# One 2048-wide model block pair on one core: job scores ahead of weight subtractions, mixed heads split one by one, 20 products moved, last gated down-projection joined

## The chip, the cores and the metric

One NeuronCore of a Trainium2 chip (trn2) runs the whole program. The metric is the device time of one execution in microseconds (us), lower is better.

## What is computed

The reference is two transformer blocks in float32 on 256 tokens of width 2048, one after the other.

```python
def reference(...):
    x = first_block(x, p, ...)
    return second_block(x, c_2, ...)

# first_block: three mixers side by side, then a gated feed-forward, then a gated projection of p
proj = rmsnorm(h) @ w_in                      # 2048 -> 4 hgrn heads, 6 fox heads, 6 moba heads of 128
h = h + concatenate([hgrn, fox, moba]) @ w_out
h = h + (gelu(conv(c @ w_gate)) * (c @ w_up)) @ w_down        # 5632 wide
h = h + sigmoid(e @ w_ple_gate) * (p @ w_ple_proj)
# second_block: modulated by silu(c) @ w_mod (12288 columns), 16 window heads of 64, 8 latent heads of 128
proj = (rmsnorm_2(x) * (1 + sc1) + sh1) @ w_in
x = x + g1 * (concatenate([swa, mla]) @ w_out)
x = x + g2 * (relu(h @ w_ff1) ** 2) @ w_ff2                   # 8192 wide
return rmsnorm_2(x)
```

## The kernel before, in words

**Split products.** Everything is feature-major: a block is 128 features by 256 tokens. Each weight is read once from HBM in units of 128 x 2048 float32 (1 MB), 384 of them, each of two halves of eight 128 x 128 tiles. ScalarE (ACT) rounds a half to fp32r (`rnd`, line 863, tile `wh`), VectorE (DVE) subtracts to get the low part (`sub`, line 1363, tile `wl`), both LOOK = 3 halves ahead of TensorE (PE) with four slots (HS = 4). Activations are split in the same way into a high and a low part (`his`, `hi_x` on ACT; `lo`, `lo_x` on DVE, lines 1493 and 1473). A tile costs PE two matmuls: high weights by the pair (512 columns, line 532) and low weights by the high part (256 columns, line 533), summed in a bank of 512 columns, of which DVE adds both halves to `x` (`add_blocks`, lines 1413 and 1415). The joined form (lines 525 to 527) makes three matmuls that sum in one half of the bank.

**The stages**, in order, with their units: A 16 (hgrn projections), B 19 (fox), C 18 (moba), out 8 and outb 8 (the two halves of `w_out`), ffn1 128 (gated feed-forward, a hardware loop of 48 halves four times in it), plep 2, down1 4 (the rest of `w_down`), pleg 16, in2 16, uq 3, ukv 2, out2 8 and out2b 8, ffn2 128.

**What runs between.** No scheduler is at work: each engine's queue is written out half by half, and semaphores join them. On DVE `half(before, after)` waits that PE has finished the half ahead, does `before` (taking the last block from PSUM), then `sub` for three halves on, then `after`. An attention job (one head) goes in steps, one step in a half, 48 steps in all: 9 in C for fox, 9 in out for moba, 19 in in2 and uq for the window heads (`swa`), 11 in out2 for the latent heads (`mla`). In a step (`job_step`) PE makes the scores of job j (line 589), the value product of j - 3 (line 598) and the transposes of j - 2 (line 607); DVE takes the scores and the maximum of j (lines 1550 to 1560) and scales the probabilities of j - 1 (lines 1567 and 1570); ACT copies out j - 3, copies the transposes of j - 2 and takes the exponential of j (line 995). All this is in `after` on DVE, behind `sub`.

**The mixed heads.** `w_out` reads `mix`, split into 16 pairs. Before `out`, ACT and DVE split the first eight at once; those eight pairs lie in `xs`, which C's products still read, so the split waits for the end of C. The last eight are split after the last job, between out and outb, and likewise in out2. The value blocks of moba are transposed by PE at the start of out, all three pairs (line 576).

**Products of the modulation.** `w_mod` is used by DVE alone: 192 products (`mods`, line 1431, 128 x 1024) of a 512 KB slice in one of two slots, each loaded by POOL's queue when the slot's last product is done.

## Time and profile before

| | |
|---|---|
| time, median of 3 runs | 2400.34 us (2397.83 to 2402.98) |
| the profiled execution | 2399.3 us, span 2397.6 us |
| granted TensorE clock, mean | 0.992 |
| PE busy | 2337.4 us (97%), 13766 matmuls |
| DVE busy | 1940.7 us (81%) |
| ACT busy | 1178.0 us (49%) |
| POOL busy | 109.0 us (5%) |
| read from HBM | 510.27 MB, 214 GB/s over the span |

The profile is of one execution. Busy times are unions of the instructions of an engine. The ends of matmuls are modelled, so the distance from one start to the next tells their pace. "Idle before" is put down to the engine that released the instruction last. Stages aren't marked in it; their places were found by counting the halves that PE finished.

### The profile page before, as it was taken

To read this page: it belongs to the slowest core of one execution; us is meant where nothing else is said; L and a number is where in the kernel's file an instruction comes from. 1 tells how busy PE (TensorE), PEld (TensorE's weight loads), DVE (VectorE), ACT (ScalarE), POOL (GpSimd) and SP (SyncE) were. 2 spreads that over 40 slices of the span, in tenths; PEclk is the share of its full clock that TensorE was granted. 3 is DMA by queue.
4 is the path that set the end of the run, shared out by engine and by line. 5 is a ranking of instruction groups with operands and counts; after the bars stand their busy time and mean duration, and the time that the engine had idled before them with its cause. 6 is when DMAs were issued, how large, how long until landed. Compare 5 with 4: busy or idle time off the path is not lost.

```text
span 2397.6 us, 38235 instructions
## 1 busy us (share of the span) xinstructions
PE 2337.4 (97%) x13766; PEld 2032.2 (85%) x13766; DVE 1940.7 (81%) x3144; ACT 1178.0 (49%) x1697; POOL 109.0 (5%) x208
## 2 busy tenths in 40 slices
PE   7999999999999999999999999999999999999997
PEld 6888787888888888888888897788988888888886
DVE  6987787889988889898989866778777777777777
ACT  5544444565545454454456666545644434434432
POOL 0000010001000000000000000000000000000000
PEclk9999999999999999999999999999999999999998
DMA  7456666458888878788775652436455545555552
GB/s 284 172 189 228 234 237 214 156 203 302 275 280 277 282 270 288 260 298 277 277 267 176 213 197 89 151 130 223 182 193 179 191 181 189 189 180 192 179 191 88
DMA packets 86244, 514.43 MB, mean 215 GB/s; under 512 B 9669, under 2 KB 10229, under 8 KB 36944
## 3 DMA queue, kind: packets, MB, share of 16 engines
q1 hardware_dynamic: 57312, 407.93, 47.6%
q0 software_dynamic: 28640, 104.24, 13.0%
q8 instruction: 95, 1.56, 0.3%
q14 instruction: 53, 0.43, 0.1%
q10 hardware_dynamic: 144, 0.26, 0.0%
HBM read 510.27 MB, written 2.13 MB: 214 GB/s over the span
## 4 chain that ended last, share of the span: by engine, by line
PE 89%; DVE 7%; ACT 2%; issue 2%; DMA 1%; SPq 0%; DVEq 0%; ACTq 0%; POOLq 0%
PE ps L532 46%; PE ps L533 23%; PE ps L530 4%; PE ps L525 2%; PE ps L526 2%; PE ps L527 2%; PE ps L529 2%; DVE wl L1363 2%; PE ps L589 2%; ACT wh L863 1%; PE ps L598 1%; DVE x L1415 1%; PE ps L617 1%; DVE modraw L1431 0%; PE ps L566 0%
## 5 line engine op out<-in xcount | busy, mean ns | idle before, releaser
L863 ACT ACTIVATE wh<-raw 128x1024 fp32r<-128x1024 f32 x768 | 810.7, 1057 | 728.9 <-PE ps L530 481.2
L1363 DVE TENSOR_TENSOR wl<-raw,wh 128x1024 fp32r<-128x1024 f32 x768 | 938.0, 1223 | 249.4 <-ACT wh L863 233.4
L532 PE MATMUL ps<-xs,wh 128*128 128x512 f32 x2907 | 1050.1, 402 | 19.7 <-DVE wl L1363 13.2
L533 PE MATMUL ps<-xs,wl 128*128 128x256 f32 x2907 | 817.9, 281 | 0.0
L532 PEld LDWEIGHTS ps<-xs,wh 128*128 128x128 f32 x2907 | 549.5, 189 | 150.2 <-DVE wl L1363 14.0
L533 PEld LDWEIGHTS ps<-xs,wl 128*128 128x128 f32 x2907 | 552.2, 190 | 10.2
L1431 DVE CUSTOM_DVE_ANT_0 modraw<-modraw,cb 128x1024 f32<-128x1024 f32 x192 | 233.2, 1218 | 4.4 <-DMA modraw<-in_wmod 4.4
L1415 DVE SCALAR_TENSOR_TENSOR x<-ps,mod,x 128x256 f32<-128x256 f32 x320 | 154.8, 484 | 88.4 <-PE ps L530 82.7
L532 PE MATMUL ps<-xc,wh 128*128 128x512 f32 x616 | 222.0, 399 | 0.0
L532 PE MATMUL ps<-hs,wh 128*128 128x512 f32 x608 | 218.8, 398 | 1.9 <-DVE x L1413 1.9
L533 PE MATMUL ps<-xc,wl 128*128 128x256 f32 x616 | 173.3, 281 | 0.0
L533 PE MATMUL ps<-hs,wl 128*128 128x256 f32 x608 | 170.6, 281 | 0.0
L532 PE MATMUL ps<-hs2a,wh 128*128 128x512 f32 x448 | 160.8, 398 | 1.6 <-DVE up L1388 0.8
L532 PE MATMUL ps<-hs2b,wh 128*128 128x512 f32 x448 | 161.0, 398 | 0.0
L525 PE MATMUL ps<-xd,wh 128*128 128x258 f32 x512 | 148.3, 290 | 3.9 <-DVE xd L1473 3.9
L526 PE MATMUL ps<-xd,wh 128*128 128x258 f32 x512 | 146.7, 287 | 0.0
L527 PE MATMUL ps<-xd,wl 128*128 128x258 f32 x512 | 145.2, 284 | 0.0
L470 POOL DMA_DIRECT2D modraw<-in_wmod x176 | 92.9, 528 | 1107.7 <-DVE modp L1431 616.2
L532 PEld LDWEIGHTS ps<-xc,wh 128*128 128x128 f32 x616 | 115.8, 188 | 28.5
L532 PEld LDWEIGHTS ps<-hs,wh 128*128 128x128 f32 x608 | 114.4, 188 | 26.3 <-issue 3.0
L533 PE MATMUL ps<-hs2a,wl 128*128 128x256 f32 x448 | 125.7, 281 | 0.0
L533 PE MATMUL ps<-hs2b,wl 128*128 128x256 f32 x448 | 125.7, 281 | 0.0
(286 smaller groups left out, 2983.0 us busy)
## 6 DMA issues: line engine op xcount, KB each, us to landing
raw<-in_w SPq DMA_DIRECT2D x383, 1024.0 KB, 5.0
modraw<-in_wmod POOLq DMA_DIRECT2D x192, 512.0 KB, 4.5
x<-in_x SPq DMA_DIRECT2D x4, 512.0 KB, 8.7
tbias<-rel_rows POOLq DMA_DIRECT2D x4, 512.0 KB, 6.0
out_dram<-mix SPq DMA_DIRECT2D x4, 512.0 KB, 2.6
raw<-in_w SPq DMA_DIRECT2D x2, 512.0 KB, 7.9
cb<-c_silu POOLq DMA_DIRECT2D x1, 1024.0 KB, 8.6
hmask<-in_hmask SPq DMA_DIRECT2D x1, 512.0 KB, 17.3
```

The costliest lines, as they stand in the source:

```text
L470: pool.dma_start(modraw[:, n:n + 1, :], a["wmod"][bass.ds(i * MOD_SLOTS + (MOD_SLOTS + n), 1), :, :] .rearrange("a p n -> p a n")).then_in ...
L525: nc.tensor.matmul(out[:, 0:N], hi[:, w], xh, start=s, stop=False)
L526: nc.tensor.matmul(out[:, 0:N], hi[:, w], xl, start=False, stop=False)
L527: m = nc.tensor.matmul(out[:, 0:N], lo[:, w], xh, start=False, stop=e)
L529: nc.tensor.matmul(out[:, 0:T], lo[:, w], xh, start=False, stop=False)
L530: m = nc.tensor.matmul(out[:, :], hi[:, w], pair, start=False, stop=True)
L532: nc.tensor.matmul(out[:, :], hi[:, w], pair, start=s, stop=e)
L533: m = nc.tensor.matmul(out[:, 0:T], lo[:, w], xh, start=False, stop=e, skip_group_check=e)
L863: nc.scalar.activation(wh[:, h % HS, :], raw[:, u % RAW, (h % 2) * 1024:(h % 2 + 1) * 1024], ACT.Copy).then_inc(s_round, 1)
L1363: nc.vector.tensor_tensor(wl[:, h % HS, :], raw[:, (h // 2) % RAW, (h % 2) * 1024:(h % 2 + 1) * 1024], wh[:, h % HS, :].bitcast(F32), ALU. ...
L1415: ins.append(nc.vector.scalar_tensor_tensor(x[:, k, :], b[:, q * T:(q + 1) * T], gate[:, k:k + 1], x[:, k, :], ALU.mult, ALU.add))
L1431: nc.vector.tensor_tensor_reduce(out=modraw[:, m % 2, :], in0=modraw[:, m % 2, :], in1=cb[:, (m % 2) * 1024:(m % 2 + 1) * 1024], scale=1.0 ...
```

## The change

DVE's `half` gets a third hook, `pre`, which runs ahead of `before` and of `sub`. All 48 job steps move there from `after`. The split of the mixed heads goes one by one: in C, two heads in each of four halves, into `xm`, a new place of 16 KB over the fox heads' projections; in out and out2 each head is split as its job ends, and the steps are packed into one half fewer. Moba's value transposes go to two halves of C and one of out.

Of the 192 products 20 leave C; each of the four loop turns in ffn1 takes 28 instead of 24, and 4 more are done in in2; the 8 of out2b go to out2. POOL's queue loads the first of the late ones ahead of its wait for the norm of in2. down1 is made with joined products, and DVE adds one 256-column half for a block instead of two.

```diff
-            def half(before=None, after=None):
+            def half(before=None, after=None, pre=None):
+                if pre:
+                    pre()
                 if before:
                     dve.wait_ge(s_used, c.val("h", c.n["h"]))
                     before()
                 sub(c.n["h"] + LOOK)
...
+            def add_joined(ks):
+                for k in ks:
+                    nc.vector.tensor_tensor(x[:, k, :], bank()[:, 0:T], x[:, k, :], ALU.add).then_inc(s_evac, 1)
+                dve.wait_ge(s_evac, c.n["b"])
...
+        xm = at("xm", [P, KB // 2, 2, T], 144, F32R)
-        XMIX = {"out": XPAIR, "out2": XPAIR[8:16] + XPAIR[0:8]}
+        XMIX = {"out": [xm[:, k, :, :] for k in range(KB // 2)] + XPAIR[8:16], "out2": XPAIR[8:16] + XPAIR[0:8]}
+        MOBA_V = {30: 0, 34: 1}
+        MIX_AT = 29
-        LATE_MODS = 14
+        LATE_MODS = 18
-        moba_steps = lambda i: share(C_H + JOB_LAG, i, MOBA_J, 2 * U_OUT)
+        moba_steps = lambda i: share(C_H + JOB_LAG, i, MOBA_J, 2 * U_OUT - 1)
+        out_taken = lambda steps, i: [j - JOB_LAG for j in steps(i) if j >= JOB_LAG]
...
-            fulls(U_C, keep(S1), lambda j: 1 + (j >= 3), fox)
+            fulls(U_C, keep(S1), lambda j: 1 <= j < 14, fox, jobs=fox_jobs)
...
+                if 0 < i - MIX_AT <= 4:
+                    for k in (2 * (i - MIX_AT) - 2, 2 * (i - MIX_AT) - 1):
+                        lo(XS["mix"] + k, XMIX["out"][k], mix[:, k, :])
...
-                unit("quad", hpairs(hs, CH_LAST), between=lambda q: early_sums(N_PLE, 2 * u + q, SUM_QUAD))
+                unit("quad", hpairs(hs, CH_LAST), between=lambda q: early_sums(N_PLE, 2 * u + q, SUM_QUAD), joined=True)
...
-                      nmod=1, m0=0)
-                downs(lambda: gate_in(CH - 1), lambda: conv(CH - 1), nmod=1, m0=CH)
-                units(CH, product, first=last_down(), h_lo_of=lambda j: h_lo(hs, j), nmod=1, m0=2 * CH)
+                      mod=lambda j: body_mods(1 + (j == 4)))
+                downs(lambda: gate_in(CH - 1), lambda: conv(CH - 1), mod=lambda j: body_mods(1 + (j == 4)))
+                units(CH, product, first=last_down(), h_lo_of=lambda j: h_lo(hs, j), mod=lambda j: body_mods(1 + (j in (1, 5))))
...
+                if 2 <= i < 10:
+                    mods(1)
...
+            def mla(i):
+                mods(i % 2)
+                for h in out_taken(mla_steps, i - 1):
+                    lo(XS["mix2"] + 8 + h, XMIX["out2"][8 + h], mix[:, 8 + h, :])
```

Three places in the queues, with line numbers of each kernel's own (1363 is 1390 in the change, 1550 is 1582, 1493 is 1525, 1396 is 1425). First DVE in late in2, from the weight subtraction ahead of the second reciprocal (of the latent norms) to the scores of a job; the number after `ps` is the bank of the scores, which alternates from job to job. Before:

```order
L1363 TENSOR_TENSOR wl_51<-raw_49,wh_50 128x1024
L1947 RECIPROCAL hvr_102<-hvr_102 128x256
L1493 TENSOR_TENSOR xs_56<-mix_57,xs_56 128x256
L1550 SCALAR_TENSOR_TENSOR prob_94<-ps5,tbias_54 128x128
L1550 SCALAR_TENSOR_TENSOR prob_94<-ps5,tbias_54 128x256
L1555 TENSOR_REDUCE small_77<-prob_94 128x1 x2
L1560 TENSOR_SCALAR small_77<-small_77,par_72 128x2
```

The same place in the change:

```order
L1390 TENSOR_TENSOR wl_51<-raw_49,wh_50 128x1024
L1999 RECIPROCAL hvr_103<-hvr_103 128x256
L1525 TENSOR_TENSOR xs_56<-mix_57,xs_56 128x256
L1582 SCALAR_TENSOR_TENSOR prob_95<-ps4,tbias_54 128x128
L1582 SCALAR_TENSOR_TENSOR prob_95<-ps4,tbias_54 128x256
L1587 TENSOR_REDUCE small_78<-prob_95 128x1 x2
L1592 TENSOR_SCALAR small_78<-small_78,par_73 128x2
```

The scores behind this subtraction were those of the same half (`ps5`) and are now those of the next (`ps4`): the job of the half has been done ahead of the subtraction.

Second DVE at the border of C and out, from the last of moba's head norms and products to the first adds of out. Before:

```order
L1431 ISA modraw_52,modp_75<-modraw_52,cb_53 128x1024
L1431 ISA modp_75 128x1
L1396 TENSOR_TENSOR tk_a_60<-ps0,tk_a_60 128x256
L1398 TENSOR_TENSOR sec_63<-tk_a_60,rstd_a_59 128x256
L1493 TENSOR_TENSOR xs_56<-mix_57,xs_56 128x256 x8
L1363 TENSOR_TENSOR wl_51<-raw_49,wh_50 128x1024
```

In the change:

```order
L1568 SCALAR_TENSOR_TENSOR sec_64<-sec_64,par_73,ps5 128x512
L1425 TENSOR_TENSOR tk_a_60<-ps0,tk_a_60 128x256
L1427 TENSOR_TENSOR sec_64<-tk_a_60,rstd_a_59 128x256
L1390 TENSOR_TENSOR wl_51<-raw_49,wh_50 128x1024
L1448 TENSOR_TENSOR x_55<-ps1,x_55 128x256 x2
```

The two products ahead of the last take of C and the eight splits behind it are gone from here.

Third DVE in down1, one half of it, from the adds to the sums of squares. Before:

```order
L1413 TENSOR_TENSOR x<-ps,x 128x256 x4
L1363 TENSOR_TENSOR wl<-raw,wh 128x1024
L1473 SCALAR_TENSOR_TENSOR xs<-x,par,xs 128x256 x2
L1502 TENSOR_TENSOR sq<-sq 128x512
L1506 TENSOR_TENSOR sqs<-sq 128x256
```

In the change:

```order
L1438 TENSOR_TENSOR x<-ps,x 128x256 x2
L1390 TENSOR_TENSOR wl<-raw,wh 128x1024
L1505 SCALAR_TENSOR_TENSOR xs<-x,par,xs 128x256 x2
L1534 TENSOR_TENSOR sq<-sq 128x512
L1538 TENSOR_TENSOR sqs<-sq 128x256
```

Two of the four adds of a half are gone.

## Rows read from the trace of the kernel before

**Rows 1.** The page: busy times, chain by engine, the products' group (busy us, mean ns, idle).

```profile
PE 2337.4 (97%) x13766; PEld 2032.2 (85%) x13766; DVE 1940.7 (81%) x3144; ACT 1178.0 (49%) x1697; POOL 109.0 (5%) x208
...
PE 89%; DVE 7%; ACT 2%; issue 2%; DMA 1%; SPq 0%; DVEq 0%; ACTq 0%; POOLq 0%
...
L1431 DVE CUSTOM_DVE_ANT_0 modraw<-modraw,cb 128x1024 f32<-128x1024 f32 x192 | 233.2, 1218 | 4.4 <-DMA modraw<-in_wmod 4.4
```

**Rows 2.** Windows: stretch, length, busy PE, PEld, DVE, ACT, POOL, PEclk, DMA share, GB/s.

```profile
780.00:840.00 60.00, 60.00 (x342) 52.15 (x341) 53.91 (x85) 24.28 (x27) 5.34 (x11) 1.00 0.80 278
1665.00:1725.00 60.00, 60.00 (x499) 59.89 (x499) 45.45 (x75) 41.79 (x70) 0.00 (x0) 1.00 0.52 194
398.40:405.20 6.80, 5.48 (x20) 4.72 (x20) 2.75 (x6) 2.43 (x4) 0.00 (x0) 0.50 0.73 243
1456.50:1459.90 3.40, 3.35 (x16) 3.35 (x17) 1.87 (x3) 2.36 (x6) 0.00 (x0) 0.50 0.01 2
1654.50:1661.30 6.80, 4.83 (x22) 4.83 (x23) 4.18 (x7) 5.79 (x7) 0.53 (x1) 0.50 0.27 84
```

**Rows 3.** Timeline of PE at the start of out: start, length in us.

```profile
397.38 1.09 PE L576 MATMUL ps<-ident,sec 128*128 128x128 f32 x8 [1.93 <-DVE sec L1398]
399.80 1.11 PE L576 MATMUL ps<-ident,sec 128*128 128x128 f32 x4 [1.32 <-ACT vt L975]
...
402.63 0.63 PE L532 MATMUL ps<-xs,wh 128*128 128x512 f32 x1
...
403.27 0.63 PE L532 MATMUL ps<-xs,wh 128*128 128x512 f32 x1
```

**Rows 4.** Waits of PE over the whole run: us in total, times, longest.

```profile
PE ps L532 <- DVE xs L1493: 2.9, 2, 1.5
```

**Rows 5.** Waits of PE, then of DVE, in 1440:1510 (late in2, uq).

```profile
PE ps L607 <- DVE prob L1570: 7.9, 6, 2.4
...
DVE wl L1363 <- ACT wh L863: 19.9, 13, 3.4
```

**Rows 6.** Timeline of DVE and PE around one of these waits.

```profile
1450.86 1.23 DVE L1363 TENSOR_TENSOR wl<-raw,wh 128x1024 fp32r<-128x1024 f32 x1 [1.50 <-ACT wh L863]
...
1454.12 0.61 DVE L1550 SCALAR_TENSOR_TENSOR prob<-ps,tbias 128x128 f32<-128x128 f32 x2
...
1456.55 0.90 PE L607 MATMUL ps<-ident,prob 128*128 128x128 f32 x3 [2.37 <-DVE prob L1570]
```

**Rows 7.** down1: waits of PE in 1243:1275; one group of DVE in 1243:1270.

```profile
PE ps L532 <- DVE x L1413: 1.9, 3, 1.4
PE ps L532 <- issue: 1.3, 1, 1.3
...
L1413 DVE TENSOR_TENSOR x<-ps,x 128x256 f32<-128x256 f32 x27 | 10.2, 417 | 0.2
```

**Rows 8.** Windows of DVE alone: busy, PEclk, DMA share, GB/s; out2b, out2, early in2.

```profile
1599.20:1646.90 47.70, 45.89 (x81) 1.00 0.61 210
1525.90:1599.20 73.30, 51.28 (x113) 1.00 0.38 130
...
1368.00:1394.00 26.00, 20.63 (x26) 1.00 0.89 317
```

**Rows 9.** Waits of PE in 1640:1665, the start of ffn2.

```profile
PE ps L525 <- DVE xd L1473: 3.9, 2, 2.5
```

**Rows 10.** Timeline of DVE and PE after a turn of the feed-forward loop.

```profile
737.30 0.42 DVE L1396 TENSOR_TENSOR tk<-ps,tk 128x256 f32<-128x256 f32 x1 [3.33 <-issue]
...
738.72 1.22 DVE L1363 TENSOR_TENSOR wl<-raw,wh 128x1024 fp32r<-128x1024 f32 x1
...
741.29 0.40 PE L532 MATMUL ps<-xc,wh 128*128 128x512 f32 x1
```

**Rows 11.** Timeline in out2: a weight subtraction, and the first matmul that reads it.

```profile
1562.74 1.23 DVE L1363 TENSOR_TENSOR wl<-raw,wh 128x1024 fp32r<-128x1024 f32 x1
...
1579.17 0.40 PE L532 MATMUL ps<-xs,wh 128*128 128x512 f32 x1
```

More of the change, by code:

```diff
@@ L672, in fox, with moba_v @@
                 head_norm(1, i - MOBA_N)
+                if i in MOBA_V:
+                    g = MOBA_V[i]
+                    pe.wait_ge(s_scl, SCALED["C"] + 2 * C_H + 2 * g + 2)
+                    if g == 0:
+                        pe.wait_ge(s_oe, J_MOBA)
+                    else:
+                        pe.wait_ge(s_hrms, 2)
+                    moba_v(g)
+            def moba_v(g):
+                for q in range(2):
+                    for t in range(2):
+                        m = nc.tensor.transpose(PS[7 - g % 2][:, (2 * t + q) * P:(2 * t + q + 1) * P],
+                                                sec[:, S1 + 2 * C_H + 2 * g + q, qt(t)], ident[:, :])
+                m.then_inc(s_vT, 1)
             for u in range(U_C):
@@ L1090, in fox @@
                 head_norm(1, S1, i - MOBA_N)
+                if i - 1 in MOBA_V:
+                    v_copy(3, MOBA_V[i - 1], 7 - MOBA_V[i - 1] % 2)
+                if 0 <= i - MIX_AT < 4:
+                    his("C", XMIX["out"][2 * (i - MIX_AT):], [mix[:, 2 * (i - MIX_AT) + k, :] for k in range(2)])
             for u in range(U_C):
@@ L1112, in eights @@
                 act.wait_ge(s_oe, jobs_done)
-                his(phase, XMIX[phase][8:], [mix[:, k, :] for k in range(8, KB)])
                 b = FIRST[phase][1] + KB
@@ L1303, in mla @@
                     job_step(J_MLA, mla_job, MLA_H, j)
-            eights("out2", None, J_END, mla, N_MLP2, "mlp2", "mix2", lambda: shift_hi(1, SH2))
+                for h in out_taken(mla_steps, i):
+                    act.wait_ge(s_oe, J_MLA + h + 1)
+                    his("out2", XMIX["out2"][8 + h:], [mix[:, 8 + h, :]])
+            eights("out2", J_END, mla, N_MLP2, "mlp2", "mix2", lambda: shift_hi(1, SH2))
             def ups2(buf, first=None):
@@ L1458, in eights @@
                         dve.wait_ge(s_oe, jobs_done)
-                    for k in range(8 if split else 8 * part, 8 * part + 8):
-                        lo(XS[name] + k, XMIX[phase][k], mix[:, k, :])
                     for i in range(2 * U_OUT):
                         half((lambda: add_blocks([i - 1], gate)) if i else None,
-                             after=lambda: (second(i) if part else between(i)))
+                             after=lambda: (second(i) if part else between(i)), pre=None if part else lambda: jobs(i))
                     tail(lambda: add_blocks([KB - 1], gate))
@@ L1967, in swa @@
                     job_step(J_SWA, swa_job, SWA_H, j)
-            fulls(U_IN2, lambda j: take_rstd("in2", j, rstd_b), lambda j: 1 <= j <= 4, swa, late=2)
+            fulls(U_IN2, lambda j: take_rstd("in2", j, rstd_b), between=swa, late=2, jobs=swa_jobs)
             def latent_take(n):
```

105 lines of the change are left out of this document (60 added, 45 removed).

## The prediction, written before the change was run

> **What bounds the kernel now.** I read the page first. TensorE (PE) is busy for 2337.4 of 2397.6 us, and 89% of the chain that ended last runs through it, so a microsecond counts only where PE stands still or runs slowly [rows 1]. Next came the windows. In the steady part of the gated feed-forward 342 matmuls, 171 pairs, fill 60 us: 0.351 us for a tile [rows 2]. That pace nothing in this change touches. What is left is the some 60 us in which PE has nothing to do, and the stretches at the lower clock. So I went through PE's waits in order of time and asked of each who releases it.
>
> Five places bear on the change. At the start of out PE stands 1.93 us, because its transposes need the last block of C, and 1.32 us more, because the third group needs a bank that ACT has to empty [rows 3]. Twice, at the middle of out and of out2, it waits for the split of mixed heads, 2.9 us together [rows 4]. In late in2 and in uq it waits six times for scaled probabilities, 7.9 us together, and there DVE itself stands 19.9 us waiting for ACT's rounding [rows 5]. In down1 it waits 1.9 us for adds, and 1.3 us for what the profile calls issue right behind them, where DVE makes its last adds too; I count both [rows 7]. At the start of ffn2 it waits 3.9 us for the low parts of the last two blocks [rows 9].
>
> **What the waits do to the clock.** The granted clock is 0.50, which is 1.2 GHz, in three stretches, 6.8, 3.4 and 6.8 us long, and each begins within or just behind one of these waits: 398.4 between the two at out, 1456.5 with the one of 2.37 us in late in2, 1654.5 with those of ffn2 [rows 2, 3, 6]. At that clock a pair takes 403.27 - 402.63 = 0.64 us, not 0.351 [rows 3], so 45% of PE's busy time there is lost: 0.45 x (5.48 + 3.35 + 4.83) = 2.5 + 1.5 + 2.2 = 6.2 us. I take it that the clock stays at 2.4 GHz once the wait ahead is gone. The Trainium skill, "TensorE: Matmul & The Clock Gate", in its terms, prices lower clock as the throttled time by one minus the ratio. By that the three stretches would be worth 8.5 us, 2.3 more than by the rows, where PE was partly idle.
>
> **The sum, part by part.**
>
> Start of out. The value transposes are spread, and the third group, which alone needs the last block, stands one half (2.8 us) after the end of C; DVE reaches that block at once, since the two products of 1.22 us ahead of it are gone [rows 1]. Both waits go, and the clock with them: 3.25 + 2.5 = 5.7 us. The work on PE is the same. In C ACT gets eight roundings more and DVE eight splits of some 0.42 us (what a 256-column operation takes in rows 10), in exchange for 20 products of 1.22 us: 24.4 us off DVE and 3.4 us onto it. Nothing there waits for longer.
>
> Mixed heads, the second eight. The last job ends in the half ahead of the border and its split is a matter of 0.4 us on each of two engines, with a half of PE's work over it: 2.9 us go. If the cover were gone, a head would cost PE 1 us.
>
> Late in2 and uq. Now DVE does the job of a half behind the subtraction, and the subtraction waits for a rounding that ACT can only do after the exponential of the job before. Rows 6 show it: the subtraction starts at 1450.86 after 1.50 us of idle time, behind it and a reciprocal the job's scores are taken at 1454.12, and PE gets its probabilities at 1456.55, 2.37 us late. With the job first this ring is cut: DVE waits for PE's scores alone, and the 19.9 us that it stood for ACT are spent behind the job. DVE's sum doesn't grow. But the two reciprocals of the latent norms and their followers still stand between two jobs, so I leave 2 us of the 7.9 standing (bounds: 0 and 4). Gain: 5.9 + 1.5 = 7.4 us.
>
> down1. DVE makes half the adds; 27 of them took 10.2 us, so some 5 us are taken off [rows 7], more than the 3.2 us that PE waited. PE pays for the joined form: 499 matmuls in 60 us are 0.361 us for a tile of three, against 0.351 [rows 2], and 64 tiles make 0.6 us. Net 2.6 us.
>
> Start of ffn2. In out2b DVE is busy 45.89 of 47.7 us, which is why it comes late with the last blocks. Eight products (9.8 us) and eight splits (3.4 us) leave it: 33 of 48. They go to out2, where 51.3 becomes 64.5 of 73.3 us [rows 8]. So the 3.9 us of waits go [rows 9], and 2.2 us of the clock: 6.1 us. If out2 were shorter, PE would wait there in turn.
>
> The moved products. Four more in early in2 bring DVE from 20.6 to 25.5 of 26 us, and DMA, at 0.89 and 317 GB/s, gets 2.1 MB more, 6.6 us at that rate [rows 8]; so the last of them come some 3.7 us late. Three halves of 2.9 us are in hand, and the stretch behind is light: nothing. Sixteen more in ffn1 are four in a turn, 4.9 us of DVE's time to the 135 us of its 48 halves, where DVE is busy 53.9 of 60 us [rows 2]: nothing either, with the doubtful place below.
>
> The sum is 5.7 + 2.9 + 7.4 + 2.6 + 6.1 = 24.7 us. Against the profiled execution's own 2399.3 us that is 2374.6 us; that execution lies 1.0 us under the median shown, so for a median I say 2375.5 us.
>
> **The rivals.**
>
> *The waits shrink but the clock does not come back.* Against it stands that all three stretches sit at a wait; for it, that the waits are only 1.3 to 2.5 us, that PE's small matmuls remain in those places, and that the mean clock of 0.992 makes some 38 us at 0.50, of which these three are 17. The 6.2 us stay: 2381.7 us.
>
> *The extra products are felt.* After each turn of the ffn1 loop DVE stands 3.33 us, and the next subtraction ends at 739.94 for a matmul at 741.29: 1.35 us in hand [rows 10]. A turn now has a second product in its third last unit; if its 1.22 us and a late load were carried over the turn, PE would wait up to 1.2 us in each of four, and the 3.7 us of in2 could come through too. Against it: DVE has some 0.5 us to spare in a unit (6 us of 60), and two units lie between. 8.5 us stay: 2384 us.
>
> *Late in2 keeps most of its waits*, since ACT, not DVE's order, sets the ring. DVE's 19.9 us behind ACT speak for it, that the jobs are taken out of that wait against it. 5.9 + 1.5 us stay: 2383 us.
>
> *Slower: the scores block the subtractions.* DVE now stands at the head of each of 48 job steps until PE has made the scores, with the adds and the subtraction for three halves on queued behind; PE's next halves and ACT's slots wait for those. The Trainium skill, in the same page's table (row on the queue depth), says that VectorE's queue is strictly first in, first out; by it nothing overtakes such a wait. Here a step holds the subtraction back by its own 2.4 us (1454.12 to 1456.55) [rows 6] and by the wait for the scores, for which I allow as much again. It decides where less than 4.8 us is in hand. In out2 a subtraction ends at 1563.97 for a matmul at 1579.17 [rows 11]: 15.2 us, so I hold it unlikely. If each step cost PE 1 us, the ring of in2 stayed and the rest came in: 2399.3 + 48 - 17.3 = 2430 us.
>
> *It does not do what it says*: the order of DVE's queue shows that it does. What could fail is that the two largest terms (7.4 and 6.1) are nil: 2388 us.
>
> **How the numbers follow.** The sum as forecast 0.58; the clock stays 0.12; late in2 stays 0.10; extra products 0.10; two terms nil, or two of these rivals together, 0.06; slower 0.04. The forecast is that of the likeliest. Its own range is 2369 to 2380: below, in2 leaves nothing (2 us), the clock is worth 8.5 us and small waits of out go; above, in2 leaves 4 us and a border 2 us. The range that holds eight in ten reaches to the rivals: 2367 to 2388 us. About 0.2%, 4.8 us, is what can be told from no change here: faster by more has all cases but the last and a remainder, 0.93; within it 0.03; slower 0.04.
>
> **What would show it.** Right: at the start of out no idle of PE over 0.5 us and a granted clock of 1.00; PE's waits on prob in late in2 under 2.5 us together; DVE's wait for wh there smaller; PE's wait on the low parts of ffn2's input gone and DVE busy some 33 us in out2b; no wait on adds in down1; C and ffn1 as long as before. Wrong: PE waits on wl anywhere behind the entry, above all in the fourth half after a loop's turn or in halves 6 to 12 of in2; DVE standing on modraw; new stretches at clock 0.50.

## The result, and the profile after

The changed kernel took 2374.76 us (median of 4 runs, 2374.1 to 2375.3), the kernel before, on the same chip, 2399.98 us (2397.83 to 2402.98): a ratio of 0.990, 95% interval 0.9887 to 0.9912. The forecast was 2375.5 us, the range 2367 to 2388. The profiled execution took 2374.66 us, its span is 2373.0 us against 2397.6 us before.

The page of the changed kernel, in the order of rows 1, with the group of the weight subtraction (busy us, mean ns, idle and what ended it) added:

```profile
PE 2327.7 (98%) x13830; PEld 2030.8 (86%) x13830; DVE 1931.1 (81%) x3128; ACT 1174.9 (50%) x1697; POOL 109.1 (5%) x208
...
PE 89%; DVE 5%; issue 3%; ACT 2%; DMA 2%; SPq 0%; DVEq 0%; POOLq 0%; ACTq 0%
...
L1390 DVE TENSOR_TENSOR wl<-raw,wh 128x1024 fp32r<-128x1024 f32 x768 | 937.9, 1222 | 205.4 <-ACT wh L883 190.5
...
L1466 DVE CUSTOM_DVE_ANT_0 modraw<-modraw,cb 128x1024 f32<-128x1024 f32 x192 | 233.9, 1220 | 13.3 <-DMA modraw<-in_wmod 12.9
```

TensorE (PE) is busy for 9.7 us less, and the span is 24.6 us shorter. So the smaller part of the gain is busy time that ran at the lower clock, and the larger one is idle time. DVE's share of the chain fell, that of "issue" and DMA rose. And the products now wait 12.9 us for their weights, not 4.4 [rows 1]: the first sign that moving them was not free.

The table counts each stage from the last matmul of the one before to its own last matmul, in us, worked out from the two traces:

```
            A      B      C     out   outb  ffn1   plep  down1 pleg  in2    uq    ukv  out2  out2b  ffn2
before    117.3  126.2  152.0  63.2  47.5  723.8  13.2  25.7  95.2  131.2  22.8   7.7  73.3  47.7  734.5
after     117.9  124.6  150.6  55.5  45.9  726.6  11.5  23.5  93.5  130.0  20.3   7.7  73.3  45.9  729.9
change     +0.6   -1.6   -1.4  -7.8  -1.6   +2.8  -1.7  -2.2  -1.7   -1.2  -2.5   0.0   0.0  -1.8   -4.6
```

Windows of the changed kernel (stretch, length, busy PE, PEld, DVE, ACT, POOL, PEclk, DMA share, GB/s) over its one stretch at 0.50 ahead of the very end, then over the starts of out and ffn2:

```profile
92.70:96.10 3.40, 3.40 (x12) 2.88 (x11) 3.37 (x5) 0.00 (x0) 0.00 (x0) 0.50 0.77 272
393.10:400.00 6.90, 6.90 (x43) 6.03 (x42) 4.93 (x9) 4.25 (x7) 0.00 (x0) 1.00 0.42 152
...
1626.70:1636.70 10.00, 10.00 (x86) 10.00 (x85) 7.37 (x12) 6.86 (x8) 0.00 (x0) 1.00 0.27 102
```

Where rows 2 had 1.2 GHz (0.50) at out and ffn2, PE is now busy all the time at 2.4 GHz (1.00), and the whole of in2 and uq has 1.00 too. The kernel before had two more such stretches, in B and in C, which the prediction did not speak of:

```profile
217.50:220.90 3.40, 3.40 (x13) 2.92 (x12) 1.71 (x3) 0.00 (x0) 0.53 (x1) 0.50 0.00 0
299.40:302.80 3.40, 3.40 (x11) 2.68 (x10) 3.20 (x6) 0.00 (x0) 1.05 (x2) 0.50 0.87 306
```

They are gone as well, and one in A has come. DVE alone, in out2b, out2 and early in2, as in rows 8:

```profile
1580.80:1626.70 45.90, 42.97 (x72) 1.00 0.54 194
1507.50:1580.80 73.30, 60.26 (x134) 1.00 0.51 175
1361.50:1394.00 32.50, 23.56 (x39) 1.00 0.82 292
```

What the change brought in stands in early in2. First PE's waits over in2 and uq (1349.5 to 1499.8); then one wait of ACT up to 1429; then DVE's timeline over two of the products (start, length, idle before and what ended it):

```profile
PE ps L786 <- ACT hsq L1293: 3.0, 1, 3.0
PE ps L603 <- ACT probT L1009: 1.4, 2, 0.7
PE ps L612 <- DVE prob L1602: 0.9, 1, 0.9
PE ps L594 <- ACT vt L1290: 0.7, 1, 0.7
...
ACT sec L976 <- DVE tb L1518: 30.1, 9, 6.7
...
1367.14 1.23 DVE L1466 CUSTOM_DVE_ANT_0 modraw<-modraw,cb 128x1024 f32<-128x1024 f32 x1 [1.61 <-DMA modraw<-in_wmod]
...
1382.03 1.23 DVE L1466 CUSTOM_DVE_ANT_0 modraw<-modraw,cb 128x1024 f32<-128x1024 f32 x1 [3.00 <-DMA modraw<-in_wmod]
```

The 7.9 us of waits for probabilities in late in2 and uq [rows 5] are down to 0.9, and that one is early. But DVE stands still for the weights of four of the eight products, 5.6 us together, and ACT, which takes the scaled block from DVE, stands 30.1 us behind DVE. The same wait in the kernel before, over 1367 to 1447, and in run 2 below, which has the jobs ahead but only four products here, over the same stage up to 1424:

```profile
ACT sec L956 <- DVE tb L1486: 0.6, 2, 0.3
```

```profile
ACT sec L976 <- DVE tb L1518: 16.3, 8, 3.0
```

So 16.3 of the 30.1 us come with the jobs' new place, which in run 2 costs PE next to nothing, and the rest with the products. Here PE waits some 5 us that it did not wait before, mostly for ACT.

### The profile page after: what moved, and what is told of

Same layout as the page of the kernel before. It is cut to its first block, busy times and chain, and to the rows that moved or that the text cites. A ratio compares the mean times of both kernels' runs of the same rounds, so it can differ in the third digit from the quotient of the medians.

```text
span 2373.0 us, 38361 instructions
## 1 busy us (share of the span) xinstructions
PE 2327.7 (98%) x13830; PEld 2030.8 (86%) x13830; DVE 1931.1 (81%) x3128; ACT 1174.9 (50%) x1697; POOL 109.1 (5%) x208
## 4 chain that ended last, share of the span: by engine, by line
PE 89%; DVE 5%; issue 3%; ACT 2%; DMA 2%; SPq 0%; DVEq 0%; POOLq 0%; ACTq 0%
PE ps L537 46%; PE ps L538 23%; PE ps L535 5%; PE ps L534 2%; PE ps L531 2%; PE ps L530 2%; PE ps L532 2%; PE ps L594 2%; DMA modraw<-in_wmod 1%; DVE wl L1390 1%; PE ps L603 1%; PE ps L622 1%; ACT wh L883 1%; PE ps L612 1%; PE ps L571 0%
## 5 line engine op out<-in xcount | busy, mean ns | idle before, releaser
L537 PE MATMUL ps<-xs,wh 128*128 128x512 f32 x2795 | 1006.1, 401 | 14.4 <-DVE wl L1390 13.4
L538 PE MATMUL ps<-xs,wl 128*128 128x256 f32 x2795 | 786.6, 281 | 0.0
L537 PEld LDWEIGHTS ps<-xs,wh 128*128 128x128 f32 x2795 | 527.2, 189 | 137.6 <-DVE wl L1390 14.2
L538 PEld LDWEIGHTS ps<-xs,wl 128*128 128x128 f32 x2795 | 530.6, 190 | 9.8
L1466 DVE CUSTOM_DVE_ANT_0 modraw<-modraw,cb 128x1024 f32<-128x1024 f32 x192 | 233.9, 1220 | 13.3 <-DMA modraw<-in_wmod 12.9
L537 PE MATMUL ps<-hs,wh 128*128 128x512 f32 x560 | 200.9, 398 | 0.0
L538 PE MATMUL ps<-hs,wl 128*128 128x256 f32 x560 | 157.4, 281 | 0.0
L537 PEld LDWEIGHTS ps<-hs,wh 128*128 128x128 f32 x560 | 105.4, 188 | 21.8
```

What stands on the lines that cost most here:

```text
L537: nc.tensor.matmul(out[:, :], hi[:, w], pair, start=s, stop=e)
L538: m = nc.tensor.matmul(out[:, 0:T], lo[:, w], xh, start=False, stop=e, skip_group_check=e)
L1466: nc.vector.tensor_tensor_reduce(out=modraw[:, m % 2, :], in0=modraw[:, m % 2, :], in1=cb[:, (m % 2) * 1024:(m % 2 + 1) * 1024], scale=1.0 ...
```

## The experiments

Twelve kernels ran, each timed in five rounds against the kernel before on the same chip (its medians on the three chips: 2399.07, 2401.52 and 2400.5 us). Ratios are to it. A difference of one or two us between two medians is within their scatter; what decides is mostly the stage that an edit touches, in the trace.

**1. The job steps behind the subtraction.**

```diff
-                if pre:
-                    pre()
                 if before:
                     dve.wait_ge(s_used, c.val("h", c.n["h"]))
                     before()
                 sub(c.n["h"] + LOOK)
+                if pre:
+                    pre()
                 if after:
                     after()
```

> The changed kernel with its job steps put back behind the weight subtraction of each half, everything else as changed. Theory (the ring of job, transposes, copy and PV is as fast as VectorE lets it): the waits for prob of late in2 and uq come back, 7.9 us of them in the trace before, and the lower-clock stretch behind them (1.5 us): about 2382 to 2384 us, with the starts of out and ffn2 as in the changed kernel. Rival (in the changed kernel the late waits went because three early in2 halves lost VectorE's lead, or because out's heads are split otherwise): the time stays within 1 us of 2374.8 and the prob waits of halves 25 to 31 stay gone.

Measured: 2376.55 us (2374.96 to 2381.77), ratio 0.9911 (0.9894 to 0.9928), 1.8 us more than the changed kernel, and not the 8 or 9 expected. PE's waits for prob over in2 and uq:

```profile
PE ps L612 <- DVE prob L1602: 5.9, 3, 3.9
```

The longest, 3.9 us, is in half 14, where DVE is late through the products (run 12, with half of them, has no such wait); one of 1.65 us is in uq, and only 0.3 us are left in halves 25 to 31. So the late waits did not come back. What did change besides: a stretch of 6.8 us at 0.50 follows the wait in half 14, uq takes 2.2 us more (22.5) and out 1.0 more (56.5). But the edit was no true undo: it left the job ahead of `after`, the half's side work, where before the change the job stood behind both.

**2. Four of in2's products back in C** (in2 again has four, in every second half).

```diff
-            fulls(U_C, keep(S1), lambda j: 1 <= j < 14, fox, jobs=fox_jobs)
+            fulls(U_C, keep(S1), lambda j: (1 <= j < 14) + (j in (1, 3, 5, 7)), fox, jobs=fox_jobs)
...
-                if 2 <= i < 10:
+                if i in (3, 5, 7, 9):
                     mods(1)
```

> The changed kernel with four of the eight products of the second in-projection moved back to stage C (which again has 17), the other four in every second half. Theory (the eight products in a row eat VectorE's lead, since each waits for its weights' transfer): the TensorE waits of halves 10 to 22 of in2, 5.3 us in the changed kernel, fall to under 1.5 us and the time to 2370 to 2371 us. Rival (these waits come from the job steps' new place ahead of the subtraction, not from the products): they stay and the time is within 1 us of 2374.8. Third possibility: the four products are felt in stage C, which gets longer by 1 us or more.

Measured: 2368.97 us (2366.86 to 2371.22), ratio 0.9872 (0.9856 to 0.9888). All of PE's waits in in2 and uq:

```profile
PE ps L603 <- ACT probT L1009: 0.6, 1, 0.6
PE ps L786 <- ACT hsq L1293: 0.4, 1, 0.4
```

In2 takes 124.9 us, 5.1 less than in the changed kernel, uq the same 20.3, C 0.3 more. So the eight products in a row caused the waits of early in2, and C takes four of them back for next to nothing.

**3. The loop's turn with 24 products**, 16 back in C.

```diff
-                units(CH, product, ..., mod=lambda j: body_mods(1 + (j in (1, 5))))
+                units(CH, product, ..., mod=lambda j: body_mods(1))
...
-            MODS, M0 = 3 * CH + 4, c.n["m"]
+            MODS, M0 = 3 * CH, c.n["m"]
```

(likewise for the two other places in the turn; C has two in units 1 to 13 and one in 14 to 16.)

> The changed kernel with 24 instead of 28 products in each turn of the first feed-forward's loop (its 16 extra ones back in stage C, halves of units 1 to 16). Theory (in the fourth half of a turn VectorE starts its instructions 5.7 us late and the extra product at its side takes away what would catch up): the two waits of 1.15 and 1.44 us in the third and fourth turn go, the VectorE stall at the turn goes back from 5.65 to about 3.3 us, and the time is about 2372 us. Rival (the stall at the turn comes from the longer loop body's code, not from the products as such, or the products are felt in C just as much): no gain, 2374 to 2376 us.

Measured: 2373.97 us (2373.07 to 2376.34), ratio 0.9895 (0.9878 to 0.9911). Ffn1 takes 723.9 us as before the change, 2.7 less than in the changed kernel, with no wait of PE left in it, and DVE's standstills at the turns are 3.2 to 3.3 us. In its profiled execution that is given back in B, C and in2 (1.6, 2.0 and 1.9 us longer), each of which has a stretch at 0.50; C also has 16 products more. The median, 0.8 us below that of the changed kernel, shows no gain by itself. The stage does: 723.8 or 723.9 us in all four kernels with 24 products in a turn, run 7's among them.

**4. The three pairs of value transposes back at the start of out.**

```diff
-        MOBA_V = {30: 0, 34: 1}
+        MOBA_V = {}
...
-                if i == 1:
+                if i == 0:
                     pe.wait_ge(s_scl, SCALED["out"])
-                    pe.wait_ge(s_vt, 4)
-                    moba_v(2)
+                    pe.wait_ge(s_oe, J_MOBA)
+                    for g in range(C_H // 2):
+                        v_transposes(3, sec[:, S1 + 2 * C_H:S1 + 3 * C_H, :], g)
```

> The changed kernel with the three pairs of value transposes of the moba heads put back at the first half of the out-projection, where TensorE waits for the head norm of the last values; the mixed heads are still split one by one. Theory (the waits there are removed by the transposes' earlier places, and the lower-clock stretch behind them follows the waits): 3.2 us of waits come back, and the granted clock falls again for 3.4 to 6.8 us, 1.7 to 3 us more: 2378 to 2381 us. Rival A (waits alone, the clock stays): about 2378 us. Rival B (what counted was the splitting of the mixed heads one by one, and the transposes fit either way): 2375 us.

Measured: 2377.07 us (2374.78 to 2380.28), ratio 0.9906 (0.9889 to 0.9922). PE's waits in out, and the window over them:

```profile
PE ps L581 <- DVE sec L1428: 1.5, 1, 1.5
PE ps L581 <- ACT vt L996: 0.2, 1, 0.2
```

```profile
392.00:396.00 4.00, 2.29 (x17) 1.70 (x16) 2.07 (x3) 2.44 (x5) 0.00 (x0) 1.00 0.00 0
```

Out takes 2.8 us more and C 0.7 less; the 0.7 is the two groups of transposes that moved. Only half of the 3.25 us of waits came back and the clock stayed at 1.00. So the rest of the wait was gone by another part of the change. My reading, which no run tests alone: no products stand in front of C's last block on DVE (0.5 us of it), and ACT has the first heads split before, so it empties the bank sooner (1.1 us). None of the three expectations fits; the truth lies between the theory and rival B.

**5. The job steps ahead, in the kernel before, and nothing else.**

```diff
             def half(before=None, after=None, pre=None):
+                if pre:
+                    pre()
                 if before:
```

(with the job steps of the four stages taken out of `after` and given as `pre`.)

> The kernel before with one part of the change alone: the job steps of all four stages run ahead of the weight subtraction and of the half's other VectorE work. Theory (this part removes the prob waits of late in2 and uq, 7.9 us, and the lower-clock stretch behind the first, 1.5 us; with only four products there, early in2 keeps VectorE's lead): 2390 to 2392 us, all else as in the kernel before. Rival (early in2 or stage C, whose 33 products stay, pay for it as the changed kernel's in2 does): 2394 to 2397 us, with new TensorE waits in halves 10 to 22 or in C.

Measured: 2387.25 us (2385.36 to 2387.92), ratio 0.9943 (0.9929 to 0.9956): 14.3 us below the kernel before by the medians, over half of the change. What the stages that it touches show is less: in2 takes 124.9 us (131.2 before) and uq 20.3 (22.8), 8.8 us together, and out, behind its third half, 0.7 less, where a wait of 0.54 us for `prob` is gone. The rest of its profiled gain is stretches at 0.50 that did not come in B and C, 1.5 and 1.8 us, and shorter ones at out and ffn2; whether the edit or chance kept them away is not shown. PE's waits in in2 and uq are those of run 2, 0.6 and 0.4 us, so the rival falls.

**6. Run 2 with the job steps of in2 and uq behind both the subtraction and the side work**, as before the change.

```diff
-            fulls(U_IN2, ..., between=swa, late=2, jobs=swa_jobs)
+            fulls(U_IN2, ..., lambda j: 1 <= j <= 4, lambda i: (swa(i), swa_jobs(i)), late=2)
```

> The run with four products of in2 in stage C (2369.0 us), with the job steps of in2 and uq alone put back where they were before the change: behind the subtraction and behind the half's other work (the 1.75 us norm multiplications and the latent scalings stand ahead of them again). Theory (it is this side work, not the subtraction, that made the jobs late: with the jobs behind the subtraction alone late in2 had no waits): the 7.9 us of waits come back in halves 25 to 31 and uq, and perhaps a lower-clock stretch of 1.5 us: 2376 to 2379 us. Rival (late in2 had its waits from something else, such as which buffers the split heads need): 2369 to 2370 us.

Measured: 2375.7 us (2374.91 to 2380.76), ratio 0.99 (0.9882 to 0.9918), 6.7 us more than run 2. PE's wait for prob in in2 and uq, then windows over the two stretches at 0.50 that came with it:

```profile
PE ps L612 <- DVE prob L1602: 7.9, 6, 2.4
```

```profile
1440.50:1443.90 3.40, 3.40 (x17) 3.27 (x16) 3.26 (x8) 0.91 (x3) 0.00 (x0) 0.50 0.00 0
1484.80:1488.20 3.40, 3.03 (x14) 3.03 (x15) 1.77 (x5) 3.35 (x9) 0.00 (x0) 0.51 0.62 258
```

The six waits of rows 5 are back to the tenth of a us. In2 and uq take 131.2 and 23.9 us, 9.9 us more than in run 2, of which 7.1 are waits and the other 2.8 fit the two stretches at 1.2 GHz (at the waits that end at 1439.1 and 1485.2). DVE's timeline there shows what the job stands behind:

```profile
1440.57 1.22 DVE L1390 TENSOR_TENSOR wl<-raw,wh 128x1024 fp32r<-128x1024 f32 x1 [1.53 <-ACT wh L883]
1441.71 1.27 DVE L2004 SCALAR_TENSOR_TENSOR sec<-sec,par,hvr 128x256 f32<-128x256 f32 x3
1443.02 0.62 DVE L1582 SCALAR_TENSOR_TENSOR prob<-ps,tbias 128x128 f32<-128x128 f32 x2
```

**7. All of it back in C but out2b's eight**: runs 2 and 3 together, C with 33 products, two a unit in units 1 to 16 and one in unit 0.

```diff
-            fulls(U_C, keep(S1), lambda j: 1 <= j < 14, fox, jobs=fox_jobs)
+            fulls(U_C, keep(S1), lambda j: 2 * (1 <= j < 17) + (j == 0), fox, jobs=fox_jobs)
```

> The changed kernel with all 20 moved products back in stage C except the eight moved from out2b to out2: in2 has 4 products, a feed-forward turn 24, stage C 33 (two a unit over units 1 to 16). In the two single runs the gains were 5.3 us of waits in in2, and in the feed-forward loop 2.7 us, given back by lower-clock stretches in B, C and in2 that the profile of the second showed. Theory (the gains add, clock stretches fall by chance on one execution or another): 2366 to 2367 us. Rival (33 products in C are felt there, or call a lower clock, 1.4 to 2 us): 2369 us, no better than with in2 alone.

Measured: 2366.78 us (2364.58 to 2370.8), ratio 0.9859 (0.984 to 0.9877). This beats both kernels: its interval lies below the changed kernel's. The window over ffn1 (columns as above) has PE busy all through, as it was not in the changed kernel:

```profile
491.90:1215.80 723.90, 723.90 (x4102) 628.40 (x4101) 653.04 (x1039) 355.66 (x483) 67.29 (x127) 1.00 0.80 278
```

```profile
494.50:1221.10 726.60, 724.01 (x4102) 628.76 (x4101) 668.77 (x1072) 352.14 (x482) 75.50 (x143) 1.00 0.82 288
```

(The second line is the changed kernel.) C takes 151.6 us, 1.0 more than in the changed kernel. In2 gives 5.1 and ffn1 2.7.

**8. The eight products of out2 back in out2b.**

```diff
                     early_adds(n, i, SQ_EIGHT + 1, 4)
+                    mods((n == N_MLP2) * (i % 2))
...
             def mla(i):
-                mods(i % 2)
```

> The changed kernel with the eight products of out2 back in its second part out2b, where they stood before the change. Theory: TensorE waits again at the start of the second feed-forward, 3.9 us for xd by the trace before, with the lower clock behind it, 2.2 us: 2380 to 2381 us. Rival (the splitting of the mixed heads one by one or the work in out2b that is left makes that start good by itself): 2375 to 2376 us.

Measured: 2384.26 us (2379.75 to 2384.7), ratio 0.9925 (0.991 to 0.994). PE's wait at the start of ffn2, and the window behind it:

```profile
PE ps L530 <- DVE xd L1506: 2.8, 2, 2.5
```

```profile
1637.70:1641.10 3.40, 3.40 (x17) 3.40 (x17) 1.67 (x3) 3.39 (x5) 0.00 (x0) 0.50 0.30 117
```

The first six halves of ffn2 take 22.96 us, against 18.14 in the changed kernel: 4.8 us, near the 6.1 expected; DVE is busy 44.6 of 46 us in out2b. The median is 9.5 us up; the rest I can't place. The profiled execution, one of the two shortest with 2380.12 us, had stretches at 0.50 in B and in2 (2.8 us longer together).

**9. The mixed heads in a block** (the last six of out, the eight of out2).

```diff
                 act.wait_ge(s_oe, jobs_done)
+                k0 = A_H + B_H if phase == "out" else 8
+                his(phase, XMIX[phase][k0:], [mix[:, k, :] for k in range(k0, KB)])
```

(and the same for the low parts on DVE; the loops over `out_taken` go.)

> The changed kernel with the last six mixed heads of out and the eight of out2 split in one block ahead of the second part, as before the change; the first ten of out stay early. Theory: TensorE waits again at the start of outb and out2b, 1.4 and 1.5 us by the trace before, 2.9 us in all, each perhaps with 0.2 us more of small waits behind it, and none of the waits calls a lower clock: 3 to 3.6 us more than the changed kernel in those two stages. Rival (VectorE's block of six is short enough now that it is hidden in out): 1.5 us, from out2b alone.

Measured: 2380.26 us (2377.21 to 2382.91), ratio 0.9914 (0.99 to 0.9928). PE's waits at the two borders, out and then out2:

```profile
PE ps L537 <- DVE xs L1524: 0.6, 1, 0.6
```

```profile
PE ps L537 <- DVE xs L1524: 2.2, 1, 2.2
```

Outb takes 0.8 us more and out2b 2.3, 3.1 together, as expected. The remaining 2.4 us of the median I put down to stages that the edit does not touch: the profiled execution, the longest of the six, has 4.5 us more in ffn1 and 3.6 in in2.

**10. The down-projection not joined.**

```diff
-                 unit("quad", ..., joined=True)
+                 unit("quad", ...)
...
-                half((lambda: add_joined((2 * i - 2, 2 * i - 1))) if i else None, ...)
+                half((lambda: add_blocks([2 * i - 2, 2 * i - 1])) if i else None, ...)
```

> The changed kernel with the last gated down-projection as before, its products not joined and its adds in pairs, all else as changed. The prediction gave joining 2.6 us, in the down-projection alone; the two traces differ by 5.6 us there: 2.2 in the down-projection, 1.7 in the projection before it and 1.7 in the stage behind it. Theory (all three come from the joining, since its smaller adds and its end set when the neighbours' waits end): 5.6 us more than the changed kernel. Rival (the neighbours' 3.4 us come from the order of VectorE's job steps and side work, which these stages share): 2.2 to 2.6 us more.

Measured: 2378.86 us (2378.03 to 2379.54), ratio 0.991 (0.9897 to 0.9923), 4.1 us more. PE's waits in plep, down1 and pleg:

```profile
PE ps L537 <- DVE x L1448: 1.7, 2, 1.4
PE ps L537 <- issue: 1.4, 1, 1.4
```

Down1 takes 2.2 and pleg 1.7 us more, 3.9 in all; plep stays at 11.5. So joining is worth 3.9 us, and plep's 1.7 come from elsewhere.

**11. The turn's last extra product two units earlier**, on run 2.

```diff
-                units(CH, product, ..., mod=lambda j: body_mods(1 + (j in (1, 5))))
+                units(CH, product, ..., mod=lambda j: body_mods(1 + (j in (1, 3))))
```

> The kernel with four products of in2 in stage C (2369.0 us), its feed-forward turn still with 28 products, but the second one of the turn's last stage at units 1 and 3 in place of 1 and 5, so that none stands in the turn's last unit. VectorE stands still at the jump back, 3.2 to 3.6 us in the runs with 24 products, 3.6 to 5.7 us in those with 28. Theory (TensorE waits there only since the product in the last unit leaves VectorE no lead for that standstill): no TensorE wait over 0.5 us at halves 131 and 179 whatever the standstill is, and 2366 to 2367 us. Rival (the standstill is longer with 28 products wherever they stand, and decides): waits of 1 to 2 us in one or two turns again, about 2369 us.

Measured: 2369.45 us (2365.67 to 2373.59), ratio 0.9872 (0.9855 to 0.9889), the same as run 2. PE's waits in ffn1:

```profile
PE ps L537 <- DVE wl L1390: 2.9, 4, 1.1
```

The theory falls: waits of 0.7 and 1.1 us stand at the third and fourth turn again. Its premise was wrong too: the product that moved stood in the third last unit of the turn, and the last unit has its one product here as in every kernel (at 856.54 us, just ahead of the copy that ends the turn's work). Ahead of both waits DVE had stood 1.2 and 1.5 us for products' weights and ended the turn's work 2.1 and 3.6 us behind PE. At the second turn it ended it 1.0 us behind, and there PE waited only 0.3 us, though DVE stood still for 5.05.

**12. Run 2 with all job steps behind the subtraction, ahead of the side work.** The edit is that of run 1.

> The kernel with four products of in2 in stage C (2369.0 us), with the job steps of all stages put behind the weight subtraction but still ahead of the half's other work. With in2's job steps behind both, its waits came back in full (2375.7 us). Theory (the side work was what made the jobs late; the subtraction of 1.2 us is not enough to do it): late in2 stays free of waits but for small ones and at uq up to 1.7 us, as in the first run with jobs behind: 2369 to 2371.5 us. Rival (the subtraction counts as much as the side work): waits over 0.6 us in four or more halves of late in2: 2374 to 2376 us.

Measured: 2369.16 us (2367.77 to 2370.32), ratio 0.9868 (0.9851 to 0.9885), the same as run 2. PE's wait for prob in in2 and uq, and DVE's for ACT over 1440 to 1500:

```profile
PE ps L612 <- DVE prob L1602: 1.9, 2, 1.6
```

```profile
DVE wl L1390 <- ACT wh L883: 10.8, 12, 1.5
```

As in run 1 only uq waits, 1.6 us. DVE still stands twelve times for ACT's rounding, and PE does not feel it. The subtraction ahead of the jobs is not free, though: against run 2, uq takes 2.2 us more and out 1.0 (waits for `prob` of 0.8 us are back there), and in2 1.1 less.

## Why the prediction was right, and where its steps were not

The time came out within 1 us of the forecast, by a sum of parts that was less good than its total. By the two traces (forecast, then measured, us):

```
start of out                      -5.7     -7.0  (first three halves; 0.7 of it is transposes now in C)
rest of out                        0       -0.75
mixed heads (outb, out2b)         -2.9     -3.4
late in2 (halves 24 to 31), uq    -7.4     -9.5
down1, with plep and pleg         -2.6     -5.6
start of ffn2 (six halves)        -6.1     -6.6
moved products in early in2        0       +5.8
moved products in ffn1             0       +2.8
A, B, C                            0       -2.4
rest of ffn2                       0       +2.0
sum                              -24.7    -24.65
```

**Start of out.** The waits and the low clock went, as said. 7.0 less the 3.25 of waits and the 0.7 of moved transposes leaves 3.05 us, but not all of it is the clock. Run 4 has the transposes in their old place at 1.00 throughout, and its first three halves take 12.5 us where the kernel before took 16.6: of these 4.1 us 1.5 are waits, so the 6.8 us at 1.2 GHz cost 2.6, near the 2.5 of my rows. The rule of the Trainium skill ("TensorE: Matmul & The Clock Gate", "Terms") that the prediction weighed, throttled time by one minus the ratio, would be 3.4 us here; the traces show less. PE was busy for 5.48 of the 6.8 us [rows 2]. That both waits needed the spread transposes was only half true: run 4 brought back 1.7 of 3.25 us. The 0.75 us in the rest of out I had at nothing: it goes with the job order, since runs 1 and 12 bring back the wait for `prob` there and run 5 takes it away.

**Mixed heads.** Right; run 9 gives 3.1 us for 2.9, though split otherwise (0.8 and 2.3), since ten of out's sixteen were early in it.

**Late in2 and uq.** The largest term was right in place and too small: I left 2 us standing, and of the waits for `prob` nothing stayed (one of 0.6 us for ACT's copy of them, in half 27, came in their place). Run 6 prices it at 9.9 us, run 5 alone at 8.8. The step that failed is the reason I gave: "with the job first this ring is cut". What I called the ring, the subtraction waiting for a rounding that waits for an exponential, is still there in run 12, twelve times in 60 us, without PE waiting; the job behind the subtraction alone costs 1.1 us in in2 and uq together (run 12 against run 2), the job behind the side work as well another 8.8 us (run 6 against run 12). What made the job late was the side work ahead of it: the reciprocals of 1.75 us, then the latent scalings, 1.27 us between subtraction and scores in run 6. Why later halves without side work wait too (28, 29 and 31) is not shown; that a job once late stays late in the ring is my reading.

**Down1.** Run 10 gives 3.9 us for my 2.6. I counted the wait "issue" of 1.3 us with it, rightly; it stands in pleg's first half, and pleg gets 1.7 us shorter by the joining. In down1 I had left 1.3 us, the waits of 1.9 less 0.6 for the joined form, and 2.2 came: the 0.6 does not show, since PE was busy for 23.80 of down1's 25.7 us before and is for 23.40 of 23.4 now. The other 1.7 us, in plep, I overlooked in the diff: `units` now runs `last`, the split of plep's own input (tile `px`), in the first half of ffn1's last unit and not in the second, behind a product. The kernel before had a wait there:

```profile
PE ps L731 <- DVE px L1831: 1.5, 1, 1.5
```

Plep takes 13.2 us, with this wait, in both kernels without that piece (before and run 5), and 11.5, without it, in all others, joined or not; the piece alone was not tried.

**Start of ffn2.** Right: 6.6 for 6.1. Run 8 shows the mechanism with one stretch of the clock in place of two, 4.8 us. DVE's busy time in out2b, though, went from 45.89 only to 42.97 us, not to 33, and in out2 from 51.28 to 60.26, not to 64.5. My subtraction forgot that DVE was behind there before, so that a part of the stage's work fell outside it. The gated adds in the same two windows show that, before and after:

```profile
L1415 DVE SCALAR_TENSOR_TENSOR x<-ps,mod,x 128x256 f32<-128x256 f32 x28 | 13.5, 481 | 1.6 <-PE ps L530 1.1
```

```profile
L1450 DVE SCALAR_TENSOR_TENSOR x<-ps,mod,x 128x256 f32<-128x256 f32 x32 | 15.4, 482 | 1.6 <-PE ps L535 0.9
```

All 32 adds of the stage now lie within it; before, four came later, and with them the xd that ffn2 waits for.

**The moved products.** This is the step that was wrong: "three halves of 2.9 us are in hand, and the stretch behind is light: nothing". Here the price was 5.8 us in in2 and 2.8 in ffn1, 8.6 us, and the rival that the products are felt had named 8.5 us and both places. In in2 I had counted DVE's lead over PE alone. But ACT hangs on DVE too (30.1 us behind `tb`, 16.3 in run 2), and what PE waits for is mostly ACT's: values, copies of probabilities and squares. Run 2 takes that back by moving four products. In ffn1, run 7 has 723.9 us with 24 in a turn; with 28, placed as in the change, it took 723.9 to 731.1 in nine profiled executions, one of them (run 6) without a wait.

At a turn two things add up: how far DVE ends the turn's work behind PE, and how long it stands still there. In the kernel before it ended it 1.0 us behind and stood 3.3 us, and PE did not wait. At the third turn of the changed kernel it ended it 1.3 us behind and stood 5.65: PE waited 1.15 us, by the standstill. At the same turn of run 12 it was the other:

```profile
852.00 1.23 DVE L1466 CUSTOM_DVE_ANT_0 modraw<-modraw,cb 128x1024 f32<-128x1024 f32 x1 [3.99 <-DMA modraw<-in_wmod]
...
867.07 0.42 DVE L1425 TENSOR_TENSOR tk<-ps,tk 128x256 f32<-128x256 f32 x1 [3.40 <-issue]
```

```profile
PE ps L537 <- DVE wl L1390: 2.6, 1, 2.6
```

The product at 852.00 is the second one of the turn's third last unit. DVE waited 3.99 us for its weights, worked from there to the turn without a pause, ended 4.9 us behind PE, and PE waited 2.6 us with a standstill of only 3.40. That is the rival's late load carried over the turn, as it had been described, and at twice its price. So the rival was right on both of its places, and in ffn1 its mechanism is one of two.

**The other rivals.** That the scores block the subtractions did not come: DVE stood for them (28.1 us at line 1582 alone, 18 times), but PE waited for `wl` only at the entry, in A as before, and at the turns of ffn1. The clock came back at all three places, and late in2 kept no wait for `prob`.

**A, B, C and the rest of ffn2.** In A and B the differences, +0.6 and -1.6 us, fit stretches at 0.50 that came or did not. In C it is one as well, but there chance is not all that could be at work: in the fourteen executions C had such a stretch in two of the four with 29 or 33 products in it and in none of the ten with 13 or 17, too few to tell. Of the 2.0 us in the rest of ffn2, 1.2 are two waits at the turns of that stage's loop; over the twelve experiments that stretch spreads by 2.3 us, though none of them touches it. The gain to go by is that of the medians, 25.2 us, and its interval is 21 to 27 us.

Of the signs that I had named, these came true: no idle time at the start of out, clock 1.00 in all three places, the waits for `prob` in late in2, for the low parts of ffn2's input and for adds gone, DVE's wait for `wh` in late in2 and uq down from 19.9 to 4.8 us. Two did not: DVE busy some 33 us in out2b, and C and ffn1 as long as before. Of those for being wrong, three did: PE waits on `wl` in the fourth half after a turn, DVE standing on `modraw`, and a new stretch at 0.50, in A. The waits in in2, from half 10 on, are for ACT's tiles and one `prob`, not for `wl`.

## What to carry to other kernels

- When a job is late, ask of everything that stands ahead of it in its engine's queue, not only of the piece that waits. Here, in in2 and uq, the order against the 1.2 us subtraction was worth 1.1 us, the order against the 1.3 to 1.8 us of side work 8.8.
- Work off the critical path that is moved into a denser stage needs the lead of every engine behind it, ACT's as well as PE's, and its transfers need room; put it where both are slack. Stage C took all twenty back for 1 us, and the kernel got 8 us faster than the change as made.
- A total that agrees proves no term. The ten lines of the sum here were off by 0.5 to 5.8 us each, and cancelled.

## What the runs showed of the hardware that was not expected

**DVE stands still at the loop's jump back, and longer with more products in the loop.** DVE's timeline of the changed kernel at the third turn, with the PE matmul that waited for its subtraction:

```profile
857.84 0.18 DVE L1908 COPY modp<-modt 128x28 f32 x1
863.67 0.42 DVE L1425 TENSOR_TENSOR tk<-ps,tk 128x256 f32<-128x256 f32 x1 [5.65 <-issue]
...
866.36 0.50 PE L537 MATMUL ps<-xc,wh 128*128 128x512 f32 x1 [1.15 <-DVE wl L1390]
```

and that of run 7:

```profile
861.61 0.42 DVE L1425 TENSOR_TENSOR tk<-ps,tk 128x256 f32<-128x256 f32 x1 [3.49 <-issue]
```

It was 3.33 us before [rows 10]. Each of the fourteen executions has three such standstills: the twelve with 24 products in the loop last 3.2 to 3.6 us, the thirty with 28 last 3.4 to 5.65. A packet of the instruction queue falls into each of these gaps. The DMA view of the changed kernel over 861.5 to 862 has one, that over 858.2 to 861.5 none; in run 7 it comes already in 859.4 to 859.9:

```profile
q14 instruction: 1, 0.01, 3.9%
```

```profile
q14 instruction: 1, 0.01, 4.0%
```

(First the changed kernel, then run 7.) DVE goes on 1.8 us behind the end of the packet in both, and 1.3 to 1.8 us behind it in all 42. So the longer standstill is a later packet: it starts 3.55 us behind DVE's last instruction of the turn, in run 7 1.40, over all 1.1 to 1.5 us with 24 products and 1.1 to 3.55 with 28. I read it as instructions that queue behind the products' transfers; the loop's longer code is the other thing in which the kernels differ. That the packet came after 1.1 us in one turn with 28 too speaks against the code's length alone; no run tested either by itself.

**The clock does not fall at every wait of a kind.** At in2's half 22, six profiled executions had a wait of 2.9 to 3.0 us for `hsq`; in five the clock then fell to 0.50, for 3.4 us in four of them, in the changed kernel's it did not. The first line is run 10, the second the changed kernel:

```profile
1433.00:1436.40 3.40, 3.10 (x7) 2.52 (x8) 2.12 (x3) 2.87 (x4) 0.00 (x0) 0.50 0.37 154
```

```profile
1428.50:1431.90 3.40, 3.07 (x19) 2.87 (x20) 2.15 (x3) 3.37 (x6) 0.00 (x0) 1.00 0.41 173
```

The wait of 1.9 us in A (near 90 us) was followed by a fall in five of the fourteen. Behind a wait of 1.5 us at out in run 4 there was none. And two falls, in B and in C, have in the kernel before no wait of PE over 0.2 us ahead of them back to 100 us. Both came there and in run 3 (where PE had waited 0.4 us just ahead of the one in C), that in B alone in run 8, and in none of these did A's come. So each such place is worth its 1.0 to 1.8 us only in some executions. The runs of one kernel scatter by 1.2 to 9.0 us, and the clock is a good part of it: of nine runs of the kernel before on one chip the fastest, 2395.38 us, had a mean granted clock of 0.995, the slowest, 2404.11 us, one of 0.991. The waits at the turns of ffn1 are another. An edit of 2 us can be judged only in its own stage of the trace.
